# A two-layer block on one core: the scan groups' operations in another order, carried states multiplied and added by head

## What is computed

```python
SSM_HEADS, SSM_HEAD_DIM, SSM_GROUPS, SSM_STATE, SSM_CHUNK = 16, 64, 4, 128, 128

xbc = silu(causal_dwconv(xbc, conv_w, conv_b))           # xs, B and C
xs, b_ssm, c_ssm = split(xbc)
...
    da_cs = jnp.cumsum((dt * a).reshape(bsz, nc, q, g, r), axis=2)
    seg = da_cs[:, :, :, None] - da_cs[:, :, None, :]
    decay = jnp.exp(jnp.where(causal, seg, -jnp.inf))
    cb = jnp.einsum('bclgn,bcsgn->bclsg', cc, bc)
    y_diag = jnp.einsum('bclsgr,bcsgrp->bclgrp', cb[..., None] * decay, xdt)
    to_end = jnp.exp(da_cs[:, :, -1:] - da_cs)
    states = jnp.einsum('bcsgn,bcsgrp->bcgrpn', bc, xdt * to_end[..., None])
    def step(carry, inp):
        st, dec = inp
        return carry * dec[..., None, None] + st, carry
    _, prev = lax.scan(step, init, (states, exp(da_cs[:, :, -1])))
    y_off = jnp.einsum('bclgn,bcgrpn->bclgrp', cc, prev) * jnp.exp(da_cs)[..., None]
    y = y_diag + y_off + xs * d_skip
yg = y * silu(z_ssm)
y_ssm = yg * rsqrt(mean(yg * yg over a group) + eps) * ssm_norm_g
```

## Time and profile before

| | us |
|---|---|
| median of 3 runs | 2765.97 |
| lowest, highest | 2765.73, 2766.19 |
| the profiled execution, its own time | 2767.61 |
| its span in the profile | 2765.8 |
| PE busy in the span | 2583.2 (93%) |
| DVE busy | 1587.1 (57%) |
| ACT busy | 1207.3 (44%) |
| POOL busy | 1101.0 (40%) |

### The profile page before, as it was taken

One profiled execution on the slowest core, in us unless ns is written; L12 is line 12 of the kernel. 1 busy time (PEld: TensorE's weight loads), 2 busy tenths in 40 slices (PEclk: granted clock), 3 DMA queues, 4 the chain that ended last, 5 costly groups with the idle time before them and its releaser, 6 DMA issues. The chain is left out here.

```text
span 2765.8 us, 33721 instructions
## 1 busy us (share of the span) xinstructions
PE 2583.2 (93%) x12986; PEld 2146.0 (78%) x12986; DVE 1587.1 (57%) x2328; ACT 1207.3 (44%) x1816; POOL 1101.0 (40%) x738
## 2 busy tenths in 40 slices
PE   5999998989999999999999999999999999979995
PEld 3788877877888887787788787777888888868884
DVE  6654887376555556666533555653666666554334
ACT  4344886244444442334433443342655656542121
POOL 0312443328877844343775312321232332235222
PEclk9999999999999999999999999999999999989997
DMA  6232001212222237442323221211111111145431
GB/s 262 71 129 92 1 1 62 76 54 92 91 84 76 92 118 273 133 161 92 109 98 115 84 77 61 67 63 61 46 53 48 47 54 46 54 153 224 157 122 61
DMA packets 75535, 260.14 MB, mean 94 GB/s; under 512 B 8400, under 2 KB 8528, under 8 KB 75376
## 3 DMA queue, kind: packets, MB, share of 16 engines
q1 hardware_dynamic: 75376, 257.98, 26.6%
HBM read 208.01 MB, written 49.94 MB: 93 GB/s over the span
## 5 line engine op out<-in xcount | busy, mean ns | idle before, releaser
L3129 POOL TENSOR_TENSOR hl<-raw,hl 128x1024 fp32r<-128x1024 f32 x147 | 368.7, 2510 | 1039.3 <-ACT hl L1265 1039.3
L583 PE MATMUL ps<-ht,hl 128*128 128x512 f32 x1552 | 638.8, 412 | 41.5 <-DVE ht L2252 9.6
L585 PE MATMUL ps<-ht,hl 128*128 128x512 f32 x1552 | 613.6, 395 | 0.0
L584 PE MATMUL ps<-ht,hl 128*128 128x512 f32 x1552 | 613.3, 395 | 0.0
L583 PEld LDWEIGHTS ps<-ht,hl 128*128 128x128 f32 x1552 | 297.1, 191 | 109.7 <-ACT wf L1927 12.9
L585 PEld LDWEIGHTS ps<-ht,hl 128*128 128x128 f32 x1552 | 295.9, 191 | 65.0
L584 PEld LDWEIGHTS ps<-ht,hl 128*128 128x128 f32 x1552 | 297.3, 192 | 55.3 <-issue 1.5
L3206 POOL TENSOR_SCALAR wf<-wf,st 128x1024 f32<-128x1024 f32 (+2 forms) x192 | 168.0, 875 | 354.6 <-DVE st L2389 293.2
L1265 ACT ACTIVATE hl<-raw 128x1024 fp32r<-128x1024 f32 x149 | 156.5, 1052 | 190.2 <-PE ps L965 66.1
L796 PE MATMUL ps<-cst,wf 128*128 128x128 f32 x1088 | 159.9, 279 | 24.5 <-DVE ht L2404 12.0
L796 PEld LDWEIGHTS ps<-cst,wf 128*128 128x128 f32 x1088 | 129.3, 143 | 65.8 <-issue 38.5
(11 more groups left out here) (272 smaller groups left out, 5361.6 us busy)
## 6 DMA issues: line engine op xcount, KB each, us to landing
raw<-in_wst SPq DMA_DIRECT2D x229, 512.0 KB, 3.8
wf<-scratch_rows SPq DMA_DIRECT2D x32, 512.0 KB, 5.2
scratch_g<-wf SPq DMA_DIRECT2D x22, 512.0 KB, 2.6
wf<-scratch_g SPq DMA_DIRECT2D x44, 256.0 KB, 4.4
wf<-in_xT SPq DMA_DIRECT2D x16, 512.0 KB, 7.6
htf<-in_wst SPq DMA_DIRECT2D x16, 512.0 KB, 15.4
wf<-in_wst SPq DMA_DIRECT2D x10, 512.0 KB, 4.5
scratch_x<-wf SPq DMA_DIRECT2D x8, 512.0 KB, 5.4
```

The source lines that it names most:

```text
L583: self.op.matmul(out, wh, xh[:, c], start=(j == 0), stop=False)
L584: self.op.matmul(out, wh, xl[:, c], start=False, stop=False)
L585: t = self.op.matmul(out, wl, xh[:, c], start=False, stop=(j == kt - 1))
L3129: self.op.tensor_tensor(K.hl[:, u * 2048 + 1024:u * 2048 + 2048], K.raw[:, i % 3 * 1024:(i % 3 + 1) * 1024], hi.bitcast(F32), ALU.subtract ...
```

## The change

Five edits, all in `ssm`:

1. PE: B's transposes are issued inside C's product, after 11 of its 16 steps, in place of behind it.
2. ACT: `decay` is cut in two, `decay_from` ("from") and `decay`. The "from" parts of heads 2 and 3 come right after B's activation, then Bt, then both decays, and C's bias and activation behind them. Decay 3 was behind the chunks.
3. DVE: the last part of the normalization comes ahead of decay 1, in place of behind it.
4. DVE: decays 2 and 3 come ahead of C's convolution; 2 was behind it and 3 behind the chunks.
5. DVE: the carried state is made by one multiply-and-add for each head (4 of 64 columns, factor from a column of the decays), in place of a multiply and an add of 256 columns with a wait between them.

```diff
@@ TensorEngine.ssm
-            self.run(self.dense(("C", g), 1, x))
+            for n, _ in enumerate(self.dense(("C", g), 1, x)):
+                if n == 10:
+                    self.to_tokens(2, [("xsilu", 8 + g)], 3, ("B", g))
+            self.empties(3, ("Bt", g))
             self.empties(1, ("xconv", 12 + g))
             late = first(g + 1)
             self.fillers = [zs(2 * g, 0), zs(2 * g + 1, 1), late]
-            self.to_tokens(2, [("xsilu", 8 + g)], 3, ("B", g))
-            self.empties(3, ("Bt", g))
             self.fill(8)
@@ ScalarEngine.ssm
-        def decay(g, q):
+        def decay_from(g, q):
             x, e_t = w(DT[q]), w((14, 22)[q // 2])
...
             self.op.activation(e_t[a, :], x[a, :], ACT.Exp).then_inc(*self.done("from", g, q))
+
+        def decay(g, q):
+            x = w(DT[q])
             self.wait_ge(*K.at("within", g, q))
             self.op.activation(x, x, ACT.Exp).then_inc(*self.done("decay", g, q))
...
+            decay_from(g, 0)
             decay(g, 0)
...
+            decay_from(g, 1)
             decay(g, 1)
...
-            conv(12 + g, 1, 3, ("C", g))
+            decay_from(g, 2)
+            decay_from(g, 3)
             self.wait_ge(*K.at("turned", ("B", g), 1))
...
             self.op.activation(w(5), K.ps[3][:, :], ACT.Copy).then_inc(*self.done("Bt", g))
             decay(g, 2)
+            decay(g, 3)
+            conv(12 + g, 1, 3, ("C", g))
             self.fill(8)
             for c in range(7):
                 self.fill(2)
-            decay(g, 3)
@@ VectorEngine.ssm
             conv(2 * g + 1, 1, 1)
+            next(side, None)
             decay(g, 1)
             self.fetch(("B", g))
-            next(side, None)
             conv(8 + g, 0, 2)
...
+            decay(g, 2)
+            decay(g, 3)
             conv(12 + g, 1, 3)
-            decay(g, 2)
             self.fill(8)
...
-                self.op.tensor_tensor(
-                    v3(K.prev[:, c + 1, :], 64), v3(K.prev[:, c, :], 64),
-                    K.decv[:, c, 4 * g:4 * g + 4].unsqueeze(2).broadcast_to([128, 4, 64]),
-                    ALU.mult).then_inc(*self.done("prev1", g, c))
-                self.wait_ge(*K.at("prev1", g, c))
                 self.wait_ge(*K.at("state", g, c))
-                self.op.tensor_tensor(K.prev[:, c + 1, :], K.ps[3][:, off:off + 256],
-                                      K.prev[:, c + 1, :], ALU.add
-                                      ).then_inc(*self.done("prev", g, c))
+                for q in range(4):
+                    o = slice(64 * q, 64 * q + 64)
+                    self.op.scalar_tensor_tensor(
+                        out=K.prev[:, c + 1, o], in0=K.prev[:, c, o],
+                        scalar=K.decv[:, c, 4 * g + q:4 * g + q + 1],
+                        in1=K.ps[3][:, off + 64 * q:off + 64 * q + 64], op0=ALU.mult, op1=ALU.add
+                        ).then_inc(*self.done("prev", g, c))
...
-            decay(g, 3)
             self.wait_ge(*K.at("decay", g, 3))
```

## The result

| | before | changed |
|---|---|---|
| median, us | 2766.08 (4 runs, 2765.73 to 2769.01) | 2739.76 (4 runs, 2734.31 to 2743.41) |
| profiled execution, its own time | 2767.61 | 2742.31 |
| its span | 2765.8 | 2740.5 |
| mean granted clock of PE | 0.975 | 0.973 |

The ratio of the runs is 0.9901 with a 95% interval of 0.9881 to 0.9921: faster, and the medians lie 26.3 us apart. The forecast was 2738 us (28.2 us won).

What follows compares the result with a forecast made beforehand. PE's waits and lower clock in the scan bound what could be won: 3.7 + 4.5 + 4.7 + 11.8 + 5.1 = 29.8, less 1.6 for POOL, 28.2 us, from 2766.0 to 2738 us; 8 in 10 range 2733 to 2748.

Steps and rivals of the forecast that it cites:

- 15 waits: PE's waits in the scan that the change touches: 22.3 us idle, with 0.16 more each 24.7 us.
- 1.6 us kept for POOL: Decays meeting POOL's operation on DVE: 0 to 0.8 us a group, taken as 0.4, so 1.6 us lost.
- Part 1: Normalization on DVE ahead of the second decay: three waits of x's transposes go, 3.7 us won at no cost.
- Part 2: B's transposes inside C's product on PE: 3.4 us sooner, their inputs ready, no wait added.
- Part 3: Decays ahead of C's convolution: waits for B's copy (4.5 us) and a PSUM bank (4.7 us) go; meeting POOL costs 0 to 2.4.
- Part 4: Carried states by head on DVE: 0.9 us a chunk, unheld by POOL; four waits of L1109 go, 11.8 us.
- A: Waits stay, smaller, from small operations' cost and POOL's delays: 2742 to 2753 us, middle 2745; chance 0.22.
- C: Slower: the new carried-state instructions wait for POOL, last state 7.3 us late, about 2769 us; chance 0.03.
- the slack of 0.3 us: End of group 1's state chain: last carried state done at 1672.4, PE wants it at 1672.7.
- D: Little comes of it, PE's time being taken by a late bank or weights: 2755 to 2766 us; chance 0.07.
- The clock: PE's lower clock behind L1109's wait in groups 1 to 3 goes with the wait: 1.7 us each, 5.1 us.
- Rival B: PE's clock stays low somewhere else, as behind the one-column sums, and 5.1 us isn't won: 2743 us; chance 0.11.

Runs made afterwards that it cites:

- e3: The kernel before with only the normalization moved ahead of decay 1: 2766.29 us, 0.9999 of before.
- e6: The changed kernel with B's transposes put back behind C's product: 2745.28 us, 0.9918 of before.
- e5: The changed kernel with C's convolution again ahead of decay 2 and decay 3 behind the states, on ACT and DVE: 2756.68 us, 0.9964 of before.
- e1: The changed kernel with carried states again by a multiply and an add of 256 columns, all orders as changed: 2755.27 us, 0.9965 of before.
- its repeat: The changed kernel run again with no edit: 2744.05 us, 0.9914 of before.
- e2: The kernel before with only the carried states made by head, orders as before: 2749.20 us, 0.9943 of before.
- e10: The kernel before with only the one-column sums issued in four pieces: 2753.18 us, 0.9951 of before.
- e8: The changed kernel with the one-column sums in four pieces between wide matmuls: 2735.55 us, 0.9887 of before.
- e9: The changed kernel with sums in pieces, C's bias ahead of decays, group 0's B transposes later, two key-product steps moved in group 3: 2729.35 us.

## Why the prediction was right, and where it was off

**The size of the prize.** 15 waits worth 24.7 us and 1.6 us kept for POOL: 23.1 us. The rest of the stretch fell by 22.5 us. Groups 1 to 3 gave, with their clock set aside, 6.5, 6.5 and 6.7 us, a little more than the 6.1 of the sum: behind a wait the next step is longer too, 1.93 us for 1.82 (1660.45 to 1662.38), and L1109's 16 products take 2.05 us at full clock behind a wait and 1.95 without. That 0.1 us a wait the sum left out.

**Part 1**: 3.7 forecast, 4.1 in e3's stretch, right, though that kernel's runs show no gain.

**Part 2**: "no wait added" failed in group 0. I had worked it out on group 1 alone. In group 0 PE reaches the transposes at 1555.8 us, and DVE's last read of the PSUM pair (L2888) ends at 1557.0. There the transposes wait 1.4 us and the third state product 0.8 us: group 0 won 2.9 us, not 5.3. e6 shows that the part gives nothing beside part 3, and e5 that alone it costs.

**Part 3**: the decays' meeting with POOL came in every group, near the upper bound of 2.4 us (5.47 us for the 16 pieces, against 15 x 0.2 + 0.28 = 3.3 unheld, so 2.2), where I had put half. In groups 1 to 3 it cost PE 0.17 us at the wait and 0.11 behind it, 0.3 us a group, where the prediction had 0.8 for the whole meeting and 0.4 in the sum. Undone it is worth 11.4 us with part 2 in place (e5), more than the 9.2 us that I had as its two terms.

**Part 4**: the step that carries the forecast. 64-column operations take 0.276 us and start on average 0.214 us apart ((2.63 - 0.28) / 11): 0.19 to 0.20 within a chunk, where the prediction had 0.2, and 0.3 from one chunk to the next. A chunk takes 0.89 us, forecast 0.9. The Trainium skill (VectorE: DVE Perf Modes, "The DRAIN you can't avoid") has the next operation start when the pipe is empty; by that the prediction got 1.1 us a chunk, and the measured rows decide against it for these operations. The same section of the Trainium skill adds that a next operation that isn't held starts earlier, which the prediction left out and these rows agree with. The Trainium skill (GPSIMD Engine Reference, Specifications, on the SBUF interfaces) has DVE contend with GpSimd where DVE reads two SBUF inputs; e1's multiplies (2.05 us beside POOL, 0.42 without) and the changed kernel's multiply-and-adds agree. Undone, 12.3 us; alone, 12.0; forecast 11.8. Rivals A and C fall: no wait at L1110 is left. (The chain had z's gate at 1.14 us, has 1.22; with that the slack of 0.3 us is 0.2, and nothing changes.) D falls with the 26 us that came. L2944 was held by POOL, to 1672.7 of the changed kernel's clock, and hid as said.

**The clock** is the term that was mis-sized: 5.1 us forecast, "with the wait, the lower clock behind it should go". In the stretch 1.7 us came back in the profile and none in its repeat. What failed is the assumption that the clock would stay elsewhere as it was: behind the first L1110 of groups 1 to 3 the clock is full as forecast, but the loss behind group 3's sums grew from 1.7 to 3.4 us (in the repeat group 2's too), and group 3's second L1110 fell to half clock behind z's wait, which cost nothing before. Rival B, the clock low somewhere else, was the true one for this term. With part 4 alone the term came in full (e2: 5.1 us). e10 suggests that the losses behind the sums and behind the waits hang together, as both went with the sums in pieces; e8's loss behind a wait and e3's group 1 speak against a simple rule, and it isn't shown. How an earlier row of sums would decide over a later wait stays open, and so does whether the moment at which a wait or a row falls decides; no run moves only that.

Sum: 28.2 forecast, 26.3 measured by the medians, 25.3 by the means of ten and 18 runs. The two profiled spans also lie 25.3 us apart: 22.5 from the waits, 1.7 from the clock in the scan, and 1.1 outside the scan, where nothing was changed. So the waits are understood, and part of the closeness in total is luck: with the 22.5 us alone the forecast would have been missed by 5.7 us.

Still open: why 30.6 to 41.1 us go to the clock ahead of the scan in profiles of the same instructions, and how much of the runs' spread that is.

## What to carry to other kernels

Where DVE and POOL work side by side on SBUF, read both timelines at once: an operation on DVE whose length is the rest of POOL's is a stall, and here reading one input from PSUM, even in four instructions for two, removed it. A wait that is worked out in one repetition must be checked in the first, where the neighbours stand differently. Where the granted clock falls behind a row of thin products, try them spread between wide ones: here it was worth 6 us in the changed kernel and 14 in the one before.

## What the runs showed of the hardware

- Sixteen one-column products (32 matmul records) in a row, 3.6 us, are in the scan nearly always (26 of 27) followed by a loss of clock, such as 3.7 us at 0.56 (before, group 1) or 5.1 at 0.50 (changed, group 3); in four pieces of 0.95 us with 0.7 us of wide matmuls between them they are followed by none (e8, e9, e10).
- PE can stand for 2.8 us without a lower clock behind it (e10, all four groups; group 0 before; group 1 of e3), or lose 1.7 us of clock behind the same wait (groups 1 to 3 before). With the sums, some 55 us earlier, in pieces the loss was gone in e10; one behind a wait of 2.4 us was left in e8.
- A stream of 128-column single-input SBUF operations on DVE (0.2 us apart) is held by a POOL operation that starts after the stream's first piece: the second piece takes 2.44 us, to the end of POOL's (all four groups of the changed kernel).
- On DVE a multiply of two SBUF inputs beside POOL takes 2.0 to 2.1 us, and an add of as many columns with one input in PSUM 0.42 (e1).
